# Expert weights in transfers of 4 MB into four slots instead of transfers of 2 MB into eight

## The chip, the cores and the metric

The kernel runs on one core of a Trainium2 chip. The metric is the time of one execution in microseconds of device time; the figure quoted for a kernel is the median of its runs. Arithmetic is float32 throughout. The compute engines are PE (matmul), DVE, ACT and POOL; SP only issues transfers from HBM and waits on semaphores.

## The reference

One inference step with two layers. Each layer first mixes 384 tokens (128 of a prompt, 256 of a sample) by pooling and two kinds of attention, and then sends them through a mixture of 16 experts, of which this is what matters here:

```python
def ec_moe(h, w_router, w_gate, w_up, w_down):
    b, n, d = h.shape
    cap = CAPACITY_FACTOR * n // N_EXPERTS
    aff = jax.nn.softmax(jnp.einsum('bnd,de->ben', h, w_router).astype(jnp.float32), axis=1)
    vals, idx = lax.top_k(aff, cap)
    xg = jax.vmap(lambda hb, ib: hb[ib])(h, idx)
    a = jnp.einsum('becd,edf->becf', xg, w_gate)
    u = jnp.einsum('becd,edf->becf', xg, w_up)
    o = jnp.einsum('becf,efd->becd', jax.nn.silu(a) * u, w_down) * vals[..., None].astype(h.dtype)
    return jax.vmap(lambda ib, ob: jnp.zeros((n, d), ob.dtype).at[ib.reshape(-1)].add(ob.reshape(-1, d)))(idx, o)
```

Each expert takes 16 tokens of the prompt and 32 of the sample, and has three weight matrices of 1024 x 1024, so a layer reads 16 x 3 x 4 MB = 192 MB of expert weights and uses each of them once.

## The kernel before

The program is written engine by engine, with semaphores set by hand. In each of the two layers (`l`) there are two stages.

The **mixing stage** takes its weights in 57 units of 1 MB (`w_mix`), loaded by SP at L580 into eight slots of the tensor `ring`. The last eight units fill slots 0 to 7: four of the output projection (`wo`, used by `project_out`, L1708), four of the modulation rows 10 and 11 (used by `mod`, L1439). Between them and the end of the stage stand the router, the choice of the tokens and the gathering of the chosen tokens (`gather`, L1803 and L1805).

The **expert stage** works on pairs of experts. Eight pairs make four groups (`NG`) of two pairs (`c` is 0 or 1). For a pair, PE runs six projections (`project`, L1813 to L1826): gate and up for the first 512 hidden columns (g = 0, 1), gate and up for the other 512 (2, 3), then down for each half of the output columns (4, 5). A projection has 16 matmuls: the contraction over 1024 rows in two halves (`h`), in each half four blocks of 128 rows (`q`) for two experts (`e`). Each half has its own block of 2 MB of weights, and PE waits on `landed` for it (L1818). After the first half PE raises `first_half_used`, after the second `bank_full`. Between the projections 3 and 4 stand transposes (L1840, L1846) and, in every second pair, the gathering for the next group; after projection 5 the results are spread back to the tokens (L1859), and DVE adds them to `x` (L1399).

The weights lie in 16 slots of 1 MB: slots 0 to 7 are `ring`, slots 8 to 15 lie in the tensor `M`, over buffers of the mixing stage (`more_ring`). A transfer of 2 MB (`load_double`, L547) fills a double slot, and the double slots are taken in a fixed order:

```python
EARLY = (8, 10, 12)
DOUBLES = EARLY + (0, 2, 4, 6) + (14,)
```

SP issues everything in program order. `load_early` issues the three transfers of `EARLY` when the attention's last value product is done, well before the expert stage. `load_group` issues the rest: the first transfer into 0, 2, 4, 6 waits until the two mixing units in that double slot are used, that into 14 until `x` is ready (`x_mixed`, `xss_ready`), and each later one, by `wait_pair`, until PE has used the half projection eight transfers before it. After the last transfer of a layer the same queue goes on with the mixing units of the next layer, the first of them into slot 7.

## Time and profile before

| | |
|---|---|
| median of 3 runs | 1880.3 us (1878.68 to 1880.63) |
| the profiled execution | 1879.76 us, its span 1878.0 us |
| PE busy | 1739.9 us, 93% of the span |
| DVE, ACT, POOL busy | 493.5, 296.2, 112.3 us |
| read from HBM | 528.73 MB |
| transfers of expert weights | 192 of 2048 KB |
| 16 DMA engines over the span | mean 283 GB/s, in the expert stages some 430 GB/s |

The page of the profile cuts the span into 40 slices of 47 us and gives the busy share of each engine in tenths. For TensorE it is not a measure of how close it is to its peak, since matmuls are pipelined. The line of the DMA shows the two stages well: low figures are mixing stages, a run of nines is an expert stage. The slice-by-slice view says how long an engine was busy; what it waited for is told by the views of single instructions and of the waits. Since the matmuls overlap, a group's time is read best from the distance between two starts.

### The profile page before, as it was taken

What the parts mean: (1) busy time and instruction counts of PE and PEld (TensorE: products, weight loads), DVE (VectorE), ACT (ScalarE), POOL (GpSimd) and SP (SyncE); (2) the same over time, 40 slices, a digit from 0 to 9 for tenths busy, and PEclk for the clock granted to TensorE, in tenths of its full rate; (3) what the DMA queues carried; (4) which work ended last, traced back from release to release, by engine and by line L of the source; (5) the groups of instructions that cost most, each with busy time, mean ns of one, the idle gap of its engine ahead of it and who ended that gap; (6) DMA issues with size and microseconds to landing.
All of it is one profiled execution on the core that took longest, in us unless ns stands there. A gap on an engine that the chain in (4) does not pass through costs nothing.

```text
span 1878.0 us, 18992 instructions
## 1 busy us (share of the span) xinstructions
PE 1739.9 (93%) x7336; PEld 811.0 (43%) x7336; DVE 493.5 (26%) x1126; ACT 296.2 (16%) x738; POOL 112.3 (6%) x152
## 2 busy tenths in 40 slices
PE   6998999999899998898889989999998999988997
PEld 3455555554434333242245555555544343323332
DVE  1345333212312111111114344332132121102111
ACT  2233222100201010010022333221011010101000
POOL 1151000000000000000012400000000000000000
PEclk9998999999999999999999989999999999999999
DMA  9451111642799999999982701117337999999997
GB/s 387 179 224 74 68 68 68 242 177 80 330 430 429 431 432 430 432 430 430 408 349 90 274 23 67 68 68 313 135 129 318 429 431 431 431 431 430 431 430 300
DMA packets 48080, 531.77 MB, mean 283 GB/s; under 512 B 5712, under 2 KB 6768, under 8 KB 9360
## 3 DMA queue, kind: packets, MB, share of 16 engines
q1 hardware_dynamic: 45328, 524.45, 67.2%
q0 software_dynamic: 1536, 5.87, 0.9%
q8 instruction: 44, 0.72, 0.1%
q10 hardware_dynamic: 1152, 0.56, 0.1%
q14 instruction: 20, 0.16, 0.0%
HBM read 528.73 MB, written 2.13 MB: 283 GB/s over the span
## 4 chain that ended last, share of the span: by engine, by line
PE 75%; DMA 19%; DVE 2%; ACT 2%; issue 1%; SPq 0%; ACTq 0%; POOL 0%; DVEq 0%; POOLq 0%
PE bank L1822 23%; DMA ring<-in_w_moe 14%; PE bank L1487 13%; PE bank L1506 7%; PE bank L1552 6%; PE bank L1708 4%; DMA M<-in_w_moe 4%; PE bank L1859 4%; PE bank L1439 2%; PE bank L1585 2%; PE bank L1805 2%; PE bank L1650 2%; PE bank L1515 1%; PE bank L1623 1%; PE bank L1530 1%
## 5 line engine op out<-in xcount | busy, mean ns | idle before, releaser
L1487 PE MATMUL bank<-hT,ring 128*128 128x384 f32 x768 | 260.7, 493 | 0.0
L1822 PE MATMUL bank<-M,hT 128*64 128x512 f32 x1024 | 228.0, 595 | 25.3 <-DMA M<-in_w_moe 22.1
L1822 PE MATMUL bank<-ring,hT 128*64 128x512 f32 x1024 | 226.3, 594 | 13.9 <-DMA ring<-in_w_moe 13.9
L1487 PEld LDWEIGHTS bank<-hT,ring 128*128 128x128 f32 x768 | 144.0, 191 | 105.5 <-issue 12.5
L1822 PEld LDWEIGHTS bank<-M,hT 128*64 128x64 f32 x1024 | 73.4, 137 | 175.8 <-issue 150.3
L1822 PEld LDWEIGHTS bank<-ring,hT 128*64 128x64 f32 x1024 | 73.0, 137 | 164.5 <-issue 147.1
L1506 PE MATMUL bank<-M,ring 128*128 128x384 f32 x384 | 134.2, 492 | 10.1 <-ACT M L757 10.1
L1822 PE MATMUL bank<-M 128*64 128x512 f32 x512 | 114.0, 595 | 10.6 <-DMA M<-in_w_moe 6.7
L1822 PE MATMUL bank<-ring,M 128*64 128x512 f32 x512 | 113.8, 595 | 7.9 <-DMA ring<-in_w_moe 7.2
L1552 PE MATMUL bank<-ring,hT 128*128 128x512 f32 (+1 forms) x288 | 117.4, 567 | 1.4 <-DVE hT L1028 1.4
L933 ACT ACTIVATE hT<-bank 128x512 f32<-128x512 f32 x32 | 19.1, 597 | 625.4 <-PE bank L1822 625.4
L1506 PEld LDWEIGHTS bank<-M,ring 128*128 128x128 f32 x384 | 71.0, 190 | 67.9 <-ACT M L757 19.9
L1859 PE MATMUL bank<-M 128*128 128x512 f32 x192 | 93.5, 622 | 0.0
L1708 PE MATMUL bank<-ring,xn 128*128 128x512 f32 x192 | 83.7, 594 | 2.9 <-DVE xn L1040 2.9
L1391 DVE TENSOR_TENSOR M<-bank,g2slot 128x512 f32<-128x512 f32 x32 | 22.1, 691 | 241.6 <-PE bank L1822 241.6
L1379 DVE SCALAR_TENSOR_TENSOR hT<-hT,bank 128x512 f32<-128x512 f32 x32 | 22.0, 687 | 228.7 <-ACT hT L933 228.7
L1552 PEld LDWEIGHTS bank<-ring,hT 128*128 128x128 f32 x288 | 54.2, 190 | 62.1 <-issue 62.1
L1384 DVE SCALAR_TENSOR_TENSOR hT<-hT,bank 128x512 f32<-128x512 f32 x32 | 22.0, 687 | 206.7 <-PE bank L1822 206.7
L604 POOL TENSOR_TENSOR rstd<-var,mhalf 128x8 f32<-128x8 f32 (+3 forms) x34 | 43.9, 1292 | 511.9 <-DVE var L955 511.9
L1399 DVE TENSOR_TENSOR x<-x,bank 128x512 f32<-128x512 f32 x96 | 65.9, 687 | 27.0 <-PE bank L1859 27.0
L1822 PEld LDWEIGHTS bank<-M 128*64 128x64 f32 x512 | 36.8, 137 | 81.6 <-issue 74.5
L1822 PEld LDWEIGHTS bank<-ring,M 128*64 128x64 f32 x512 | 35.9, 137 | 79.3 <-issue 67.8
(223 smaller groups left out, 1524.2 us busy)
## 6 DMA issues: line engine op xcount, KB each, us to landing
M<-in_w_moe SPq DMA_DIRECT2D x96, 2048.0 KB, 30.1
ring<-in_w_moe SPq DMA_DIRECT2D x96, 2048.0 KB, 30.1
ring<-in_w_mix SPq DMA_DIRECT2D x110, 1024.0 KB, 6.7
ring<-in_w_mix SPq DMA_DIRECT2D x4, 576.0 KB, 3.7
M<-in_counts POOLq DMA_DIRECT2D x2, 768.0 KB, 12.7
x<-in_x_sample SPq DMA_DIRECT2D x1, 1024.0 KB, 8.1
M<-in_b_mod POOLq DMA_DIRECT2D x2, 512.0 KB, 7.0
g2slot<-in_b_mod POOLq DMA_DIRECT2D x2, 512.0 KB, 10.5
```

Source lines behind the costliest of these rows:

```text
L604: nc.gpsimd.tensor_tensor(rstd[:, c0:c0 + n], var[:, c0:c0 + n], mhalf[:, 0:n], ALU.pow)\
L1399: V.tensor_tensor(xs, xs, bank[b][:, :], ALU.add).then_inc(bank_read[b], 1)
L1439: ins = mm(ps[32 * q:32 * q + 32, :], cs[:, 4 * h + q, :], w[:, q, :], start=(h == 0), stop=(h == 1))
L1487: ins = mm(ps[:, 0:TOK], w[:, q, (j % 4) * P:(j % 4 + 1) * P], hT[:, 4 * h + q, :], start=(h == 0 and q == 0), stop=(h == 1 and q == 3))
L1506: ins = mm(ps[:, 0:TOK], w[:, q, (j % 4) * P:(j % 4 + 1) * P], y[:, q, :], start=(q == 0), stop=(q == 3))
L1552: ins = mm(ps[:, 0:n], hT[:, 4 * h + q, t * P:(t + 1) * P], w[:, q, 0:n], start=(h == 0 and q == 0), stop=(h == 1 and q == 3))
L1585: ins = mm(ps[:, 0:TOK], w[:, q, g * P:(g + 1) * P], hT[:, 4 * h + q, :], start=(h == 0 and q == 0), stop=(h == 1 and q == 3))
L1650: ins = mm(ps[:, :], ckvT[:, k, t * P:(t + 1) * P], w[:, k, h * 512:(h + 1) * 512], start=(k == 0), stop=(k == 1))
L1708: ins = mm(ps[:, :], merged[:, 4 * h + q, t * P:(t + 1) * P], w[:, q, :], start=(h == 0 and q == 0), stop=(h == 1 and q == 3))
L1805: ins = mm(v[:, :, CP:USED], xn[:, t, kb * P:(kb + 1) * P], chosen(t, CP, USED), start=(t == 1), stop=(t == 2))
L1822: ins = mm(bank[b][64 * e:64 * e + 64, :], lhs(e, 4 * h + q), w[:, q, :], start=(h == 0 and q == 0), stop=(h == 1 and q == 3))
L1859: mm(bank[b][:, :], selT[:, t * P:(t + 1) * P], osb[:, n * 512:(n + 1) * 512], start=True, stop=True).then_inc(bank_full[b], 1)
```

## The change

One transfer now carries both halves of the contraction of a projection, for both experts: 4 MB, 32 KB on each of the 128 partitions where it was 16 KB. It fills four slots of 1 MB. There are four such places, taken in the order 8, 0, 4, 12; only the first (slots 8 to 11) is loaded early. PE waits once for a projection and raises only `bank_full` at its end, and SP waits for the whole projection four transfers back. The host lays the weights out so that a transfer's part for one partition is in one piece. The matmuls, their order and the number of bytes are as before.

```diff
--- before.py
+++ after.py
@@ -29,9 +29,9 @@
 UNIT = 2048
 RING = 8
 RINGX = 16
-EARLY = (8, 10, 12)
-DOUBLES = EARLY + (0, 2, 4, 6) + (14,)
-ND = len(DOUBLES)
+EARLY = (8,)
+QUADS = EARLY + (0, 4, 12)
+ND = len(QUADS)
 NEG = -1e30
 NLOAD = 8
 NPOW = 17
@@ -258,10 +258,10 @@
 
 
 LANDED = [sum(slot_of(u) == s for u in UNITS) for s in range(RINGX)]
-LANDS = [c + (12 * NP // ND if s % 2 == 0 else 0) for s, c in enumerate(LANDED)]
+LANDS = [c + (6 * NP // ND if s in QUADS else 0) for s, c in enumerate(LANDED)]
 FIRSTS = [u for u in UNITS if u[2] == 0 and u[0] in ("mod", "seg", "gate", "wo")]
 FIRST_AT = {u: n for n, u in enumerate(FIRSTS)}
-HALVES = len(FIRSTS) + 6 * NP
+HALVES = len(FIRSTS)
 
 
 def last_group(u):
@@ -524,14 +524,10 @@
             sp.dma_start(x[:, 0, :], a["x_prompt"][0]).then_inc(x_in, 16)
             sp.dma_start(x[:, 1:3, :], a["x_sample"][0].rearrange("(t p) d -> p t d", p=P)).then_inc(x_in, 16)
 
-            def wait_pair(l, gr, c, j):
-
-                g, h = j // 2, j % 2
-                if h == 0:
-                    sp.wait_ge(first_half_used, l * HALVES + len(FIRSTS) + 6 * (2 * gr + c) + g + 1)
-                else:
-                    b = (0, 1, 2, 3, 5, 6)[g]
-                    sp.wait_ge(bank_full[b], in_pair(l, b, gr, c, PROJECT[b]) + 1)
+            def wait_pair(l, gr, c, g):
+
+                b = (0, 1, 2, 3, 5, 6)[g]
+                sp.wait_ge(bank_full[b], in_pair(l, b, gr, c, PROJECT[b]) + 1)
 
             def wait_mixing(l, u):
 
@@ -540,34 +536,34 @@
                 else:
                     wait_full(sp, l, last_group(u))
 
-            def load_double(l, gr, j):
-
-                s = DOUBLES[j % ND]
-                both = more_ring[:, s - RING:s - RING + 2, :] if s >= RING else ring[:, s:s + 2, :]
-                sp.dma_start(both, a["w_moe"][l, 2 * gr + j // 12, j % 12].rearrange("p (e n) -> p e n", e=2))\
+            def load_quad(l, gr, j):
+
+                s = QUADS[j % ND]
+                four = more_ring[:, s - RING:s - RING + 4, :] if s >= RING else ring[:, s:s + 4, :]
+                sp.dma_start(four, a["w_moe"][l, 2 * gr + j // 6, j % 6].rearrange("p (e n) -> p e n", e=4))\
                     .then_inc(landed[s], 16)
 
             def load_early(l):
 
                 wait_full(sp, l, ("o", NM - 1))
                 for j in range(len(EARLY)):
-                    load_double(l, 0, j)
+                    load_quad(l, 0, j)
 
             def load_group(l, gr, first):
-                for j in range(len(EARLY) if first else 0, 24):
-                    s = DOUBLES[j % ND]
+                for j in range(len(EARLY) if first else 0, 12):
+                    s = QUADS[j % ND]
                     if j >= ND:
-                        wait_pair(l, gr, (j - ND) // 12, (j - ND) % 12)
+                        wait_pair(l, gr, (j - ND) // 6, (j - ND) % 6)
                     elif not first:
-                        wait_pair(l, gr - 1, 1, j + 12 - ND)
+                        wait_pair(l, gr - 1, 1, j + 6 - ND)
                     elif s >= RING:
                         sp.wait_ge(x_mixed, 3 * (l + 1))
                         sp.wait_ge(xss_ready, 6 * (l + 1))
                     else:
                         for u in UNITS[-RING:]:
-                            if slot_of(u) in (s, s + 1):
+                            if s <= slot_of(u) < s + 4:
                                 wait_mixing(l, u)
-                    load_double(l, gr, j)
+                    load_quad(l, gr, j)
 
             for l in range(L):
                 for n, u in enumerate(UNITS):
@@ -575,7 +571,7 @@
                     if n >= RING:
                         wait_mixing(l, UNITS[n - RING])
                     elif l > 0:
-                        wait_pair(l - 1, NG - 1, 1, 12 - ND + DOUBLES.index(s - s % 2))
+                        wait_pair(l - 1, NG - 1, 1, 6 - ND + QUADS.index(s - s % 4))
                     width = unit_width(u)
                     sp.dma_start(ring[:, s, 0:width], a["w_mix"][l, n, :, 0:width]).then_inc(landed[s], 16)
                     if n == AFTER_ATTENTION:
@@ -1812,17 +1808,15 @@
 
                     def project(g, b, lhs):
                         begin_pair(b, PROJECT[b])
+                        j = 6 * c + g
+                        s = QUADS[j % ND]
+                        pe.wait_ge(landed[s], 16 * (l * LANDS[s] + LANDED[s] + gr * (12 // ND) + j // ND + 1))
                         for h in range(2):
-                            j = 12 * c + 2 * g + h
-                            s = DOUBLES[j % ND]
-                            pe.wait_ge(landed[s], 16 * (l * LANDS[s] + LANDED[s] + gr * (24 // ND) + j // ND + 1))
                             for q in range(4):
                                 for e in range(2):
-                                    w = expert_slot(s + e)
+                                    w = expert_slot(s + 2 * h + e)
                                     ins = mm(bank[b][64 * e:64 * e + 64, :], lhs(e, 4 * h + q), w[:, q, :],
                                              start=(h == 0 and q == 0), stop=(h == 1 and q == 3))
-                            if h == 0:
-                                ins.then_inc(first_half_used, 1)
                         ins.then_inc(bank_full[b], 1)
 
                     if c == 0:
@@ -1901,11 +1895,11 @@
 
 def expert_units(v):
 
-    out = np.empty((L, NP, 6, 2, P, 2, 4, 512), np.float32)
+    out = np.empty((L, NP, 6, P, 2, 2, 4, 512), np.float32)
     for g, (name, c) in enumerate((("w_gate", 0), ("w_up", 0), ("w_gate", 1), ("w_up", 1), ("w_down", 0), ("w_down", 1))):
         w = v[name].reshape(L, NP, 2, 2, 4, P, 2, 512)[:, :, :, :, :, :, c]
-        out[:, :, g] = w.transpose(0, 1, 3, 5, 2, 4, 6)
-    return out.reshape(L, NP, 12, P, 2 * UNIT)
+        out[:, :, g] = w.transpose(0, 1, 5, 3, 2, 4, 6)
+    return out.reshape(L, NP, 6, P, 4 * UNIT)
 
 
 def kernel(**inputs):
```

On SP's queue the filling of the slots at the start of the first expert stage reads as follows, before (names: `w_moe` are the expert weights, `ring` slots 0 to 7, `M` slots 8 to 15; `bank_full` is raised by PE at the end of a projection or another group of matmuls):

```order
L547 DMA ring<-in_w_moe 128x4096 [waits bank_full2,first_half_used]
L547 DMA ring<-in_w_moe 128x4096 [waits bank_full5,first_half_used]
L547 DMA ring<-in_w_moe 128x4096 [waits bank_full6,first_half_used]
L547 DMA ring<-in_w_moe 128x4096 [waits bank_full2,first_half_used]
L547 DMA M<-in_w_moe 128x4096 [waits xss_ready,x_mixed]
L547 DMA M<-in_w_moe 128x4096 [waits first_half_used]
L547 DMA M<-in_w_moe 128x4096 [waits bank_full0]
```

and with the change:

```order
L543 DMA ring<-in_w_moe 128x8192 [waits first_half_used,bank_full5,bank_full2]
L543 DMA ring<-in_w_moe 128x8192 [waits first_half_used,bank_full2,bank_full6]
L543 DMA M<-in_w_moe 128x8192 [waits xss_ready,x_mixed]
L543 DMA M<-in_w_moe 128x8192 [waits bank_full0]
L543 DMA ring<-in_w_moe 128x8192 [waits bank_full1]
```

Four transfers into `ring` have become two, each waiting for four mixing units, and the first transfer into a reused place waits for `bank_full0` (the whole first projection) where it waited for its first half.

On PE the last projections of a pair (the first pair of the layer is shown; the slots differ from pair to pair) read before:

```order
L1822 MATMUL bank<-M 64x512 [waits landed12,bank_read6]
L1822 MATMUL bank<-M 64x512 x7
L1822 MATMUL bank<-ring,M 64x512 [waits landed0]
L1822 MATMUL bank<-ring,M 64x512 x7
```

and with the change:

```order
L1818 MATMUL bank<-ring,M 64x512 [waits landed0]
L1818 MATMUL bank<-ring,M 64x512 x15
```

Both pieces are projection 5 with its 16 matmuls: the wait for the second half is gone, and the first matmul now waits for all of the 4 MB.

On SP's queue the last expert transfer of a layer and what follows it read before:

```order
L547 ISA [waits bank_full1]
L547 DMA M<-in_w_moe 128x4096
L584 REGISTER_ALU
L584 COMPARE_AND_BRANCH
L580 DMA ring<-in_w_mix 128x2048 [waits first_half_used]
```

and with the change:

```order
L543 ISA [waits bank_full1]
L543 DMA M<-in_w_moe 128x8192
L580 REGISTER_ALU
L580 COMPARE_AND_BRANCH
L576 DMA ring<-in_w_mix 128x2048 [waits bank_full5]
```

The next layer's first mixing unit waited for the first half of projection 5 of the last pair, and now waits for the end of projection 4 (`bank_full5`).

## Rows read from the trace of the kernel before

**Rows 1.** The page: DMA share and rate in 40 slices

```profile
DMA  9451111642799999999982701117337999999997
GB/s 387 179 224 74 68 68 68 242 177 80 330 430 429 431 432 430 432 430 430 408 349 90 274 23 67 68 68 313 135 129 318 429 431 431 431 431 430 431 430 300
```

**Rows 2.** PE's groups from 650 to 920 us: line, operands, count, busy, idle before them

```profile
L1822 PE MATMUL bank<-M,hT 128*64 128x512 f32 x320 | 71.8, 595 | 11.1 <-DMA M<-in_w_moe 11.1
L1822 PE MATMUL bank<-ring,hT 128*64 128x512 f32 x318 | 70.7, 595 | 7.0 <-DMA ring<-in_w_moe 7.0
```

**Rows 3.** Issues of w_moe on SP, six stretches: start us, length

```profile
458.77 17.79 SPq L547 DMA_DIRECT2D ring<-in_w_moe  x4
...
467.45 0.33 SPq L547 DMA_DIRECT2D ring<-in_w_moe  x1
...
476.66 0.37 SPq L547 DMA_DIRECT2D M<-in_w_moe  x1
...
497.67 0.33 SPq L547 DMA_DIRECT2D M<-in_w_moe  x1
...
501.11 0.33 SPq L547 DMA_DIRECT2D M<-in_w_moe  x1
...
1429.44 0.33 SPq L547 DMA_DIRECT2D M<-in_w_moe  x1
```

**Rows 4.** PE at the end of each expert stage, in order of time

```profile
925.42 3.65 PE L1822 MATMUL bank<-ring,M 128*64 128x512 f32 x16 [1.33 <-DMA ring<-in_w_moe]
930.14 3.65 PE L1822 MATMUL bank<-M 128*64 128x512 f32 x16 [1.07 <-DMA M<-in_w_moe]
933.73 6.00 PE L1859 MATMUL bank<-M 128*128 128x512 f32 x12
939.65 1.92 PE L1439 MATMUL bank<-ring,cs 128*32 128x512 f32 x16
...
1861.84 3.65 PE L1822 MATMUL bank<-M 128*64 128x512 f32 x16 [1.08 <-DMA M<-in_w_moe]
```

**Rows 5.** Stretches: length, PE, PEld, DVE, ACT, POOL busy, PE clock, DMA share, GB/s

```profile
520.00:900.00 380.00, 353.50 (x1609) 130.16 (x1605) 67.76 (x116) 27.19 (x58) 6.87 (x14) 1.00 1.01 430
10.00:20.00 10.00, 6.22 (x27) 2.80 (x28) 2.88 (x6) 4.54 (x8) 0.87 (x1) 1.00 1.01 427
931.00:944.00 13.00, 10.58 (x42) 3.00 (x38) 4.82 (x7) 3.39 (x7) 0.00 (x0) 1.00 1.00 421
```

**Rows 6.** PE before and at the first projection of the stage, in order of time

```profile
481.99 0.29 PE L1755 MATMUL bank<-const,M 16*128 16x16 f32 x2 [3.40 <-DVE M L1318]
...
493.98 2.37 PE L1822 MATMUL bank<-M,hT 128*64 128x512 f32 x10 [1.58 <-DVE hT L1369]
```

**Rows 7.** The same view by stretches: the clock around those gaps, and the stage's end

```profile
480.00:485.00 5.00, 0.71 (x4) 0.65 (x5) 4.30 (x11) 0.00 (x0) 0.44 (x1) 0.74 0.99 421
485.00:490.00 5.00, 5.00 (x28) 5.00 (x28) 0.16 (x1) 1.40 (x4) 0.54 (x2) 0.57 0.76 324
...
925.00:930.00 5.00, 3.65 (x16) 1.26 (x16) 0.00 (x0) 0.00 (x0) 0.00 (x0) 1.00 0.68 292
```

**Rows 8.** SP's waits: total us, times, longest; and first mixing units of layer 1

```profile
SPq L547 <- PE bank L1822: 741.4, 176, 20.6
...
929.10 1.99 SPq L580 DMA_DIRECT2D ring<-in_w_mix  x4
```

**Rows 9.** PE between projections: a pair with gathering, and the last pair of a layer

```profile
680.46 0.65 PE L1840 MATMUL bank<-const,hT 128*128 128x128 f32 x4
...
688.15 10.52 PE L1822 MATMUL bank<-ring,M 128*64 128x512 f32 x48
...
702.03 5.79 PE L1859 MATMUL bank<-M 128*128 128x512 f32 x12
...
914.22 0.66 PE L1840 MATMUL bank<-const,hT 128*128 128x128 f32 x4
...
916.91 7.17 PE L1822 MATMUL bank<-ring,M 128*64 128x512 f32 x32 [0.36 <-ACT M L936]
```

## The prediction

> **What bounds the kernel now.** I began with the slices of the page. In the expert stages the 16 DMA engines are at nine tenths or more in every slice and move 429 to 432 GB/s, in the mixing stages they are mostly idle [rows 1]. The groups of PE in the later part of an expert stage say the same from the other side: the idle time in front of the projections is put down to the landing of `w_moe` [rows 2]. PE is busy 353.50 of 380 us there, and the figure counts overlapping matmuls [rows 5], so the high share of PE on the page does not make PE the bound. The stage ends when the stream of weights ends.
>
> Next, where that stream starts and ends. SP fills the eight double slots of layer 0 by 476.66, then stands until 497.67, when PE has used the first half projection, and issues the next at 501.11 [rows 3]. A half projection therefore takes 501.11 - 497.67 = 3.44 us and a whole one 6.88; PE's own row shows 3.65 for 16 records, whose modelled end overlaps the next group [rows 4]. From that first reuse at 497.67 to the start of the last half projection at 930.14 pass 432.47 us, and in layer 1 from 1429.44 to 1861.84 another 432.40 [rows 3, 4]. That is 88 transfers of 2 MB (96 of a layer less the 8 that fill the slots), 4.91 us each with the first one's latency in it. Twice the same to 0.1 us, and at an unbroken 429 to 432 GB/s between [rows 1]: each layer is *first reuse of a slot + 432.4 us + what PE does after the last landing*. The change touches all three.
>
> **The start of the stream: +3.44 us a layer.** The slots before the first reuse hold the same 16 MB. What frees a place is now the whole first projection. PE reaches it as before, since it waits there for DVE and not for weights (493.98, after 1.58 us for DVE) [rows 6], and slots 8 to 11 are loaded long before. So the first reuse is issued 3.44 us later, at 501.11 by the clock of the old trace.
>
> The filling itself changes and costs nothing as long as it is done by then. Two MB less are loaded early; the load of slots 0 to 3 waits for all of `wo` and so goes out at 467.45 where the first went at 458.77 [rows 3]; the loads of 4 to 7 and 12 to 15 go out at about 476.2 and 476.7 behind the same two waits as before. Twelve MB at 430 GB/s are 29.3 us, so the engines are done at 497 to 498, still 3 us ahead of 501.11. PE wants slots 0 to 3 at 493.98 + 6.88 = 500.9 (landed by 478), 4 to 7 at 507.7 (landed by 488) and 12 to 15 at 514.6 (landed by 499). The cover is thin for the engines and wide for PE; were the fill later than 501, the stream would start at its end instead, and each microsecond would count.
>
> **The end of the stream: +3.44 us a layer.** The last block of a layer is projection 5 of the last pair. Before, its first half ran at 925.42 while the second was on its way, and only one half, 3.44 us, followed the last landing [rows 4]. Now both halves follow it, 6.88 us. Projection 4 is no obstacle: its weights land 9.75 us before, and projection 3 with the 2.7 us of transposes behind it (914.22 to 916.91) [rows 9] is done by then to within 0.2 us. What comes after, L1859 and DVE's additions, moves along whole. In layer 0 the next layer's first `mod` stands right behind on PE (939.65) [rows 4] and needs mixing units that were issued at 929.10 [rows 8], after a small hole in the DMA (share 0.68) [rows 7]. Those now wait for projection 4 alone, which is done 2.9 us before the last landing, so the hole closes (about 1.6 us of DMA) and the units are there earlier relative to PE; PE did not wait for them before, so nothing is gained either. The later arrival of `x` is what counts, and all of layer 1's mixing stage moves with it.
>
> **The rate of the stream: -1.75 us a layer.** A transfer row per partition is 32 KB where it was 16. Rows of 16 KB go at 430 GB/s over 380 us, and at 431 in several slices of the page [rows 1, 5]; rows of 8 KB (`w_mix`) go at 427 in one stretch and at 421 in another, both with the DMA full [rows 5]. So doubling the row saved 0.8 to 2.2% of the time per byte. If what is saved is a fixed cost of a row or of a transfer, the next doubling saves half of that, 0.4 to 1.1% of the 430 us that 44 transfers take: 1.75 to 4.7 us a layer. If the saving came from something else there may be none. I take 1.75, from the stretch of 427, because it is the more careful of the two rows and the other includes the moment at which the expert weights give way to mixing units on the queue; the ends are 0 and 4.7. The Trainium skill ("DMA: Bandwidth & Descriptors", Specifications and Where 436 GB/s comes from) puts the ceiling of the ports into SBUF at 435.2 GB/s; the trace agrees as far as it goes, no slice being above 432. By that ceiling as an estimate the saving could be at most 1.1%, 4.6 us a layer.
>
> **What else moves, and costs nothing.** SP issues 96 transfers fewer, of 0.33 us each, on an engine that waited 741.4 us for PE in this place [rows 3, 8]. PE loses 96 waits and as many semaphore raises. In the middle of the stage SP may have three transfers of 9.75 us ahead of the one PE works on, 29.2 us of cover for any break of PE. The longest break is in a pair with gathering: 7.7 us from the transposes to the next projection, then 5.8 us of L1859 behind projection 5 [rows 9]. Stepped through with landings every 9.75 us, projection 3 ends 6.9 us behind its landing, projection 4 11.7, projection 5 8.8, the next pair's first 11.8. That stays far below 29.2, so the stream does not break. While PE is the slower one, early in the stage, SP's reuses follow PE's pace, which is faster than the stream, as before.
>
> **The sum.** Own time of the profiled execution 1879.76, plus 2 x (3.44 + 3.44 - 1.75) = +10.3, gives 1890.0 us. That execution lies 0.5 us below the median of the three runs, which is within their spread, so 1890 stands for the median as well. A measurement can tell about 0.2%, 3.8 us.
>
> **The rivals.**
>
> *Faster: larger rows pay in full.* If the jump from 421 to 430.5 GB/s (the middle of 430 and 431) repeats, the 430 us shrink by 2.2%, 9.5 us a layer, against 6.88 added: 2 x (6.88 - 9.5) = -5.2, 1874.5 us. It decides from a rate of about 437 GB/s on, where the two cancel. For it speaks only the row of 421; against it the row of 427 and that a fixed cost halves with each doubling. By the ceiling on the page named above it could not happen at all. Chance 0.07.
>
> *A wash.* A saving between 0.7 and 1.6% with nothing against it gives 1876 to 1884 us, within 0.2%. It needs the upper bound of the rate and a start that loses less than a half projection. Chance 0.09.
>
> *Slower still: PE's clock falls in the longer gaps.* Waiting once per 4 MB, PE stands 9.75 - 6.88 = 2.9 us in front of a projection where it stood 1.3 or less in front of a half [rows 2, 4]. In the old trace a gap of 3.40 us, with little work around it, was followed by 0.74 and 0.57 of the clock, that is, by time at 1.2 GHz [rows 6, 7], while gaps of 1.3 left it at 1.00 [rows 5]. In mid-stage the slower projections would eat up their own gap. At the end the last projection, at half clock all through, costs 6.88 more a layer: up to 1890 + 13.8 = 1903.8, and half of that if it recovers midway. Against it: the work between the gaps is dense, that around 482 was not (0.71 us of matmuls in 5) [rows 7]. The Trainium skill ("TensorE: Matmul & The Clock Gate", Why this matters for your kernels) names long idle gaps between bursts of matmuls as what lowers the clock; if 2.9 us counts as long, it gives the second of these times, and the rows of this trace have no single gap of that length before dense work. Chance 0.11.
>
> *Slower still: three transfers ahead are too few.* If PE's breaks plus SP's waits did reach 29 us, the stream would stop once per group; 3 us in three groups of two layers are 18 us, 1908. The steps above speak against it. Chance 0.03.
>
> **How the numbers follow.** My forecast has the other 0.70; its own range is 2 x (6.88 - 4.7) = +4.4 to 2 x 6.88 = +13.8, so 1884 to 1893.5. The range takes in part of the wash below (1882) and a clock that falls and recovers in the last projection above, 1897. Left out are the faster case, half of the wash and half of the two slower ones, 0.2 in all. Faster by over 0.2%: 0.07 and a little for what I have not seen, 0.08. Within 0.2%: 0.11, with the lower edge of my own range. Slower: 0.81.
>
> **What the profile after would show.** Right: SP's first transfer into a reused place comes some 3.4 us later after PE's first projection begins than before (7.1 us behind it in place of 3.7); from there to the start of the last projection 429 to 432.5 us; 6.9 us from that start to L1859; gaps of 2.9 us in front of projections late in the stage, clock 1.00; a rate of 431 to 435 GB/s; the DMA without the hole before the mixing units. Wrong: a rate outside that span, which moves the sum by 8.6 us for each per cent; a clock below 1 in the expert stage; a DMA share under 0.98 in mid-stage; or PE waiting for slots 12 to 15 at the start.

## The result, and the profile after

The changed kernel takes 1887.04 us (median of 7 runs, 1885.29 to 1888.38), the kernel before 1880.3 in the same comparison (7 runs, 1878.49 to 1883.71). The ratio is 1.0037, with a 95% interval of 1.0026 to 1.0049. It is slower by 5 to 9 us, as forecast, and by less than the 10.3 us of the sum. A second comparison of the same two kernels (`after_again`, below) gave 1.0047, 1.0034 to 1.0060. The profiled execution after took 1888.38 us, its span 1886.6.

Lines have moved: the projections are now L1818 (before L1822), the spreading back to the tokens L1853 (L1859), the transfers of expert weights L543 (L547), `mod` L1435 (L1439).

The page of the profile after, its rates in 40 slices, beside [rows 1] (its expert weights come in 96 transfers of 4096 KB):

```profile
GB/s 383 181 223 74 68 67 67 256 127 40 390 432 432 432 433 434 433 434 431 404 327 91 273 23 67 68 67 267 134 100 389 431 432 433 434 434 433 432 432 266
```

The slices of an expert stage read 431 to 434 where they read 429 to 432. The view by stretches of the same kernel (length, busy time of PE, PEld, DVE, ACT and POOL, granted clock, DMA share, GB/s) answers to [rows 5] and [rows 7]:

```profile
520.00:900.00 380.00, 355.34 (x1593) 132.66 (x1591) 67.12 (x115) 27.17 (x58) 6.86 (x14) 0.98 1.00 433
...
910.00:915.00 5.00, 2.38 (x8) 0.83 (x8) 0.69 (x1) 0.60 (x1) 0.00 (x0) 0.83 0.97 419
...
930.00:935.00 5.00, 4.13 (x22) 1.45 (x20) 0.69 (x1) 0.00 (x0) 0.00 (x0) 1.00 0.58 206
```

Three things are to be seen: 433 GB/s for 430; a granted clock of 0.98 where it was 1.00, with a stretch at 0.83 that holds the end of a wait and the start of the projection behind it (part of it at 2.4 GHz, part at 1.2 GHz); and a DMA share of 0.58 where the expert weights give way to the mixing units. Layer 1 reads the same 0.98 and 433 between 1460 and 1840 us. Below, a *dip* is such a fall of the clock within one projection. Now the two ends of the stream in order of time. SP's first transfer into a reused place, and PE at the first projection, for [rows 3] and [rows 6]:

```profile
501.98 0.33 SPq L543 DMA_DIRECT2D M<-in_w_moe  x1
```

```profile
494.86 7.09 PE L1818 MATMUL bank<-M,hT 128*64 128x512 f32 x32 [1.67 <-DVE hT L1365]
```

PE at the end of the stage, for [rows 4] and the last part of [rows 9]:

```profile
903.23 7.09 PE L1818 MATMUL bank<-M,hT 128*64 128x512 f32 x32 [2.14 <-DMA M<-in_w_moe]
912.94 8.78 PE L1818 MATMUL bank<-ring,hT 128*64 128x512 f32 x32 [2.62 <-DMA ring<-in_w_moe]
...
924.34 7.09 PE L1818 MATMUL bank<-ring,M 128*64 128x512 f32 x32 [0.36 <-ACT M L932]
932.30 7.09 PE L1818 MATMUL bank<-M 128*64 128x512 f32 x32 [0.87 <-DMA M<-in_w_moe]
939.32 6.00 PE L1853 MATMUL bank<-M 128*128 128x512 f32 x12
```

The reuse comes 501.98 - 494.86 = 7.12 us behind the first projection (before 497.67 - 493.98 = 3.69). From it to the last projection pass 932.30 - 501.98 = 430.32 us (before 432.47). From that start to L1853 pass 7.02 us (before 933.73 - 930.14 = 3.59). In all 444.46 us lie between the first projection and L1853, against 439.75 before: +4.71 in this layer. Layer 1 gives 444.38 against 439.67, again +4.71. So the trace accounts for +9.4 us in the two expert stages. The measure *first projection to L1859 (L1853)* is used for every kernel below, since the rest of the time scatters by itself and its code hardly differs between them.

### The profile page after: what moved, and what is told of

It reads as the page before. It is cut to its first block, busy times and chain, and to the rows that moved or that the text cites. A ratio compares the mean times of both kernels' runs of the same rounds, so it can differ in the third digit from the quotient of the medians.

```text
span 1886.6 us, 18662 instructions
## 1 busy us (share of the span) xinstructions
PE 1751.1 (93%) x7336; PEld 821.2 (44%) x7336; DVE 493.9 (26%) x1126; ACT 295.9 (16%) x738; POOL 112.2 (6%) x152
## 4 chain that ended last, share of the span: by engine, by line
PE 74%; DMA 20%; DVE 2%; ACT 2%; issue 1%; SPq 0%; ACTq 0%; POOL 0%; DVEq 0%; POOLq 0%
PE bank L1818 22%; DMA ring<-in_w_moe 16%; PE bank L1483 13%; PE bank L1502 7%; PE bank L1548 6%; PE bank L1704 4%; PE bank L1853 4%; DMA M<-in_w_moe 3%; PE bank L1435 2%; PE bank L1581 2%; PE bank L1801 2%; PE bank L1646 2%; PE bank L1511 1%; PE bank L1619 1%; PE bank L1526 1%
## 5 line engine op out<-in xcount | busy, mean ns | idle before, releaser
L1818 PE MATMUL bank<-M,hT 128*64 128x512 f32 x1024 | 241.1, 627 | 30.2 <-DMA M<-in_w_moe 26.9
L1818 PE MATMUL bank<-ring,hT 128*64 128x512 f32 x1024 | 227.1, 597 | 8.3 <-DMA ring<-in_w_moe 8.3
L1818 PEld LDWEIGHTS bank<-M,hT 128*64 128x64 f32 x1024 | 80.1, 143 | 187.5 <-issue 174.4
L1818 PEld LDWEIGHTS bank<-ring,hT 128*64 128x64 f32 x1024 | 75.7, 138 | 157.1 <-issue 149.8
L1818 PE MATMUL bank<-ring,M 128*64 128x512 f32 x512 | 113.3, 595 | 8.1 <-DMA ring<-in_w_moe 7.4
L1818 PE MATMUL bank<-M 128*64 128x512 f32 x512 | 113.1, 594 | 7.3 <-ACT M L932 3.9
L1853 PE MATMUL bank<-M 128*128 128x512 f32 x192 | 93.6, 622 | 0.0
L1818 PEld LDWEIGHTS bank<-ring,M 128*64 128x64 f32 x512 | 36.6, 137 | 78.7 <-issue 67.6
L1818 PEld LDWEIGHTS bank<-M 128*64 128x64 f32 x512 | 37.1, 137 | 77.1 <-issue 74.4
```

The source lines that it names most:

```text
L1818: ins = mm(bank[b][64 * e:64 * e + 64, :], lhs(e, 4 * h + q), w[:, q, :], start=(h == 0 and q == 0), stop=(h == 1 and q == 3))
L1853: mm(bank[b][:, :], selT[:, t * P:(t + 1) * P], osb[:, n * 512:(n + 1) * 512], start=True, stop=True).then_inc(bank_full[b], 1)
```

## The experiments

Each kernel's stage length is read off its trace as above, layer 0 and layer 1. "Mixing" is the time from the start of the span to the first projection of layer 0 plus that from L1859 to the first projection of layer 1. Ratios are to the kernel before, timed on the same chip.

| kernel | stage 0, stage 1, us | mixing, us | GB/s | ratio (95% interval) |
|---|---|---|---|---|
| before | 439.75, 439.67 | 986.0 | 430.6 | |
| changed | 444.46, 444.38 | 985.2 | 432.6 | 1.0037 (1.0026 to 1.0049) |
| after_again | 444.34, 444.55 | 983.2 | 432.6 | 1.0047 (1.0034 to 1.0060) |
| e1_wait_whole | 446.76, 448.32 | 983.2 | 430.6 | 1.0081 (1.0067 to 1.0095) |
| e5_rows16 | 448.07, 448.22 | 982.8 | 430.6 | 1.0082 (1.0065 to 1.0099) |
| e6_rows8 | 444.07, 444.16 | 984.3 | 426.3 | 1.0049 (1.0035 to 1.0064) |
| e2_tail | 441.67, 441.76 | 982.1 | 432.8 | 1.0022 (1.0012 to 1.0032) |
| e3_start | 444.20, 444.72 | 982.4 | 432.3 | 1.0046 (1.0033 to 1.0060) |
| e8_start_loop | 442.16, 444.07 | 986.6 | 432.5 | 1.0045 (1.0028 to 1.0062) |
| e4_both | 442.29, 440.09 | 981.6 | 432.4 | 1.0011 (1.0002 to 1.0020) |
| e9_both_loop | 441.07, 439.81 | 986.7 | 432.7 | 1.0002 (0.9993 to 1.0012) |
| e7_warm | 450.78, 450.77 | 984.8 | 432.5 | 1.0112 (1.0095 to 1.0129) |
| e12_early | 440.78, 440.99 | 984.0 | 432.3 | 1.0003 (0.9994 to 1.0012) |
| e13_early_warm | 439.83, 439.88 | 982.8 | 432.2 | 1.0001 (0.9992 to 1.0009) |

(GB/s: from 20 us behind the first reuse to 20 us before the last projection's start, the mean of the two layers; the last digit moves by 0.1 to 0.3 with the way in which packets at the edges are counted.)

**e1_wait_whole: the waits of the change without its transfers.** In the kernel before, PE waits for both halves first, and SP for the whole projection:

```diff
                         for h in range(2):
                             j = 12 * c + 2 * g + h
                             s = DOUBLES[j % ND]
                             pe.wait_ge(landed[s], ...)
+                        for h in range(2):
+                            s = DOUBLES[(12 * c + 2 * g + h) % ND]
                             for q in range(4):
...
-                if h == 0:
-                    sp.wait_ge(first_half_used, l * HALVES + len(FIRSTS) + 6 * (2 * gr + c) + g + 1)
-                else:
-                    b = (0, 1, 2, 3, 5, 6)[g]
-                    sp.wait_ge(bank_full[b], in_pair(l, b, gr, c, PROJECT[b]) + 1)
+                b = (0, 1, 2, 3, 5, 6)[g]
+                sp.wait_ge(bank_full[b], in_pair(l, b, gr, c, PROJECT[b]) + 1)
```

Expected:

> The kernel before, its 2 MB transfers and eight slots kept, but PE waits for both halves of a projection before its first matmul, and SP takes a place again only after the whole projection. The theory (a late start and a late end of the stream, 3.44 us each and layer, less a rate that the larger rows raise) expects all of the loss and none of the gain: 2 x 6.88 = +13.8 us, 1894, with 430 to 431 GB/s in mid-stage, the first reuse 7.1 us behind PE's first projection and 6.9 us from the last landing to L1859. If the loss were due to the four places or the size of the transfers, this kernel would stay at 1880. If the rate has nothing to do with the row size, it comes out where the changed kernel did, at 1887.

Measured: 1893.77 us against 1878.56, +15.2. Stage 0 grew by 7.0 us (two half projections, 6.88, were expected), stage 1 by 8.65. The rate did not move. Both ends show in its trace, here the last projection of each layer (L1821 are its projections, L1858 the spreading):

```profile
931.82 3.65 PE L1821 MATMUL bank<-ring,M 128*64 128x512 f32 x16 [2.82 <-DMA M<-in_w_moe]
...
938.84 3.59 PE L1858 MATMUL bank<-M 128*128 128x512 f32 x7
```

```profile
1869.60 5.31 PE L1821 MATMUL bank<-ring,M 128*64 128x512 f32 x16 [2.63 <-DMA M<-in_w_moe]
...
1878.28 1.98 PE L1858 MATMUL bank<-M 128*128 128x512 f32 x4
```

In layer 0 the last projection takes 7.02 us, in layer 1 8.68: its first half began at a lowered clock, 5.31 us for 3.65. So the waits alone cost what the theory says, and the 1.66 us more is the price of a dip where it falls on the last projection.

**e5_rows16 and e6_rows8: what the rate hangs on.** e5 is the changed kernel with each 4 MB in HBM as two pieces of 16 KB per partition:

```diff
-                sp.dma_start(four, a["w_moe"][l, 2 * gr + j // 6, j % 6].rearrange("p (e n) -> p e n", e=4))\
+                sp.dma_start(four.rearrange("p (h e) n -> p h (e n)", h=2),
+                             a["w_moe"][l, 2 * gr + j // 6, j % 6].rearrange("h p n -> p h n"))\
                     .then_inc(landed[s], 16)
```

> The changed kernel, each 4 MB still one transfer into the same four slots, but laid out in HBM as two pieces of 16 KB for each partition instead of one of 32 KB. If the rate gain is a cost per row (per packet), mid-stage falls back from 432.6 to 430.6 GB/s and the stream of each layer grows by 2 us: about +4 us against the changed kernel. If it is a cost per transfer (its end on each of the 16 engines), the rate stays at 432.6 and so does the time.

e6 is the kernel before with each 2 MB as two pieces of 8 KB:

```diff
-                sp.dma_start(both, a["w_moe"][l, 2 * gr + j // 12, j % 12].rearrange("p (e n) -> p e n", e=2))\
+                sp.dma_start(both, a["w_moe"][l, 2 * gr + j // 12, j % 12].rearrange("e p n -> p e n"))\
                     .then_inc(landed[s], 16)
```

> The kernel before with its transfers of 2 MB, each now two pieces of 8 KB for a partition instead of one of 16 KB. From 430.6 GB/s with 16 KB and 432.6 with 32 KB a fixed cost of 5.6 ns per row follows (0.0225 us on each 2 MB for four rows of an engine fewer). Eight rows more then make 4.915 us in place of 4.870 per transfer: 426.6 GB/s, 4.0 us more a layer, 8 us over the kernel before. If the gain of the larger row was peculiar to 32 KB, the rate stays at 430.6 and the time too.

The view by stretches, first of e5, then of e6:

```profile
520.00:900.00 380.00, 353.38 (x1579) 131.61 (x1579) 67.13 (x115) 27.17 (x58) 6.86 (x14) 0.98 1.01 431
```

```profile
520.00:900.00 380.00, 350.06 (x1593) 128.62 (x1591) 67.78 (x116) 27.19 (x58) 6.87 (x14) 1.00 1.01 426
```

e5 kept the size and number of the transfers and fell back to the old rate: the gain belongs to the row of 32 KB, not to the transfer of 4 MB. Its stage is 448.1, with a dip on the last projection in both layers (its own +4 us over the changed kernel had left the dips out; measured were +6.7, of which two dips are 3.4). Without the dips it is 446.4, against e1's 446.7: the change from the other side, where the coarse waits cost some 14 us and the longer rows give 4.3 back. That its time, 1893.75, is e1's to the tenth is chance, since e1 had the dip in one layer only. e6 came out at 426.3 GB/s where 426.6 was worked out, its stage 4.4 us longer a layer (4.0 expected), 1887.32 us. Both runs also put the pieces of a row at other places in HBM, so length and place are not separated; for the length speaks that the rate of the third size was foretold from the other two. Three sizes of row lie on one line, with a fixed cost of about 5.8 ns per row on its DMA engine (worked out in the last section).

**e2_tail: the last 4 MB of a layer in two transfers.**

```diff
-                    load_quad(l, gr, j)
+                    if last and j == 11:
+                        for h in range(2):
+                            load_half(l, gr, j, h)
+                    else:
+                        load_quad(l, gr, j)
...
                         for h in range(2):
+                            if h and type(gr) is int and gr == NG - 1 and c == 1 and g == 5:
+                                pe.wait_ge(landed[14], 16 * (l + 1))
```

> The changed kernel, with the last 4 MB of each layer as two transfers of 2 MB, for whose second PE waits between the halves. The theory expects 3.44 us a layer back: 1887.0 - 6.9 = 1880.2, with the last half projection 3.6 us before L1859. If the end of the stage does not bound (PE late for other reasons), nothing comes back: 1887.

Measured: 1882.4 us, ratio 1.0022; the stage is 2.7 us shorter than the changed kernel's, not 3.44. The trace says why (L1833 are its projections, L1868 the spreading):

```profile
909.94 7.09 PE L1833 MATMUL bank<-ring,hT 128*64 128x512 f32 x32 [0.93 <-DMA ring<-in_w_moe]
...
919.65 7.09 PE L1833 MATMUL bank<-ring,M 128*64 128x512 f32 x32 [0.36 <-ACT M L945]
926.56 7.04 PE L1833 MATMUL bank<-M 128*64 128x512 f32 x32
933.53 6.00 PE L1868 MATMUL bank<-M 128*128 128x512 f32 x12
```

The last projection no longer waits. Projection 4, still one block of 4 MB, is in front of it, and from its start two whole projections run to the end, 13.88 us. It cannot start before its weights land (919.51; the row names ACT, which was done at the same moment), 9.7 us ahead of the last landing (929.19); so L1868 stands at least 13.88 - 9.7 = 4.2 us behind the last landing, against some 7.0, and 2.8 us is all that this repair can give.

**e3_start and e8_start_loop: the first reuse by halves.** e3 writes the first group of PE out so that its first half projection can release a place; e8 splits the fifth transfer of every group and leaves the loop as it is:

```diff
+                    if j == ND:
+                        sp.wait_ge(first_half_used, l * HALVES + len(FIRSTS) + gr + 1)
+                        load_half(l, gr, j, 0)
+                        wait_pair(l, gr, 0, 0)
+                        load_half(l, gr, j, 1)
+                        continue
```

> The changed kernel, with the first reused place filled by two transfers of 2 MB, the first issued after the first half projection. The stream of the changed kernel stands from 498.8 to about 502.5 us, so starting 3.44 us earlier just closes that hole: the theory expects 3.2 to 3.4 us a layer back, 1880.4. If the stream has slack in it and its start does not matter, 1887.

> The start repair of e3_start once more, but the first group of PE is not written out: every group splits its fifth transfer, so that PE keeps its loop. e3 gave nothing back; its trace shows 9 reads of 16 KB of instructions in mid-stage where the changed kernel has 5, with a landing 0.5 to 1.1 us late behind several of them. The theory (extra instruction reads hold up one of the 16 DMA engines and with it the whole stream by 0.6 us each) expects them back at 5 and first projection to L1859 at 442.4 us a layer in place of 444.4 (the hole that can be closed is 1.9 to 2.3 us), some 4 us under the changed kernel. If the start of the stream simply does not matter, 444.4 again.

In both, the reuse is issued 3.69 us behind the first projection, as in the kernel before. SP's first two transfers into a reused place in e8_start_loop, where the first projection starts at 496.15:

```profile
499.84 3.76 SPq L552 DMA_DIRECT2D M<-in_w_moe  x2
```

e3 gained 0.3 us in layer 0 (444.20) and lost 0.3 in layer 1 (444.72, with a dip of 1.5 us on its last projection), e8 gained 2.3 us in layer 0 (442.16) and, with a dip on its last projection (8.71 us in place of 7.02), 0.3 in layer 1. A bound of some 2 us, where 3.4 was expected, comes from the fill. In the changed kernel the records of the DMA show the last of the fill's packets over at 501.00 and the next stream's first at 502.94, a hole of 1.94 us, and only the hole can be closed, however early the reuse is issued. In the ten stages that reuse a whole place behind such a fill (the changed kernel twice, e2, e5 and e7) it is 1.5 to 3.2 us. The expectation of e3 had it from 498.8 to 502.5: that is when most of the engines stand, but the last one works until 501.00. Why e3 lost the gain again is shown only in part. Its PE program has one group more written out in place of a pass of the loop, and the DMA view from 520 to 900 us counts 9 reads of instructions (0.15 MB) in e3 and 5 (0.08 MB) in e8, as in the changed kernel.

Landings in e3's layer 0 are 9.7 us apart, but 10.8 at 549.6, 10.2 at 869.7 and 10.8 at 899.8, each 3 to 7 us after a read of 16 KB of instructions (546.4, 864.0, 892.9). With the loop restored the extra reads are gone, and stage 0 is 2.0 us shorter, stage 1 0.8 when the dips are taken off. Four reads of 0.6 us each, all on the engine that is last, would make 2.4. But a read alone does not delay a landing: in the changed kernel no landing behind its 5 reads is more than 0.1 us late, and in e8's layer 1, with the loop, one is (11.1 us for 9.7, at 1486.2). The records do not name the engine either, so this stays a possible cause and not a shown one. In the times of the whole kernels (1886.98 and 1887.45) the difference is lost in the mixing stages, which took 982.4 us in e3's trace and 986.6 in e8's.

**e4_both and e9_both_loop: both repairs.** e4 is e2 and e3 together, e9 the loop form of both (its last transfer is split in every group).

> The changed kernel with both repairs at once. The theory says that the two losses add and that the rate gain of 2.15 us a layer is then left alone: 1887.0 - 13.5 = 1873.5, about 7 us under both kernels (4.3 us of the rate and what the medians differ from the trace). If the two repairs share their gain (the one hides the other), about 1880.

> Both repairs in loop form. The theory expects the two to add now: 442.4 less the 2.7 us that the tail repair gave, 439.7 a layer from the first projection to L1859, the same as the kernel before. If the repairs share their gain, 441.7.

e4: 1881.0 us, stages 442.3 and 440.1. e9: 1879.25 us, 441.1 and 439.8, where 439.7 was expected; ratio 1.0002. The two repairs add: 2.3 and 2.8 us in layer 0, where e9 gained 3.4 with a dip of 1.4 in it, and 2.0 (e8's dip taken off) and 2.6 in layer 1, where it gained 4.6. With them the kernel is level with the one before. The two layers of e9 differ by 1.26 us, and projection 3 of the last pair shows why, behind the same gap once with a dip and once without; e4's 442.29 and 440.09 have the same cause:

```profile
911.66 8.51 PE L1841 MATMUL bank<-ring,hT 128*64 128x512 f32 x32 [2.63 <-DMA ring<-in_w_moe]
...
1844.04 7.09 PE L1841 MATMUL bank<-ring,hT 128*64 128x512 f32 x32 [2.62 <-DMA ring<-in_w_moe]
```

Once the tail is repaired, PE waits for no weights between a dip in this projection and the end of the stage, so the dip is no longer hidden. The forecast for e4, 1873.5, was wrong in its sizes: 6.9 us for each repair, where 4 to 5 and 5.5 were there to be had.

**e7_warm: keeping the clock up.** Three further matmuls stand in front of the waits of projections 2 and 3; they compute nothing that is used.

```diff
+                        for k in range(3 if g in (2, 3) else 0):
+                            mm(bank[b][64:128, :], xn[:, 0, 0:64], xn[:, 1, 0:512], start=True, stop=True)
                         pe.wait_ge(landed[s], ...)
```

> The changed kernel, with three further matmuls into the free bank in front of the waits of projections 2 and 3 of each pair, whose result the projection overwrites; nothing of the output depends on them. In the changed kernel the projection behind the longest gap takes 8.7 us in place of 6.9 at a granted clock that dips to about 0.83. The theory says that the dip is hidden, since the next weights land only after it: with it gone (clock 1.00 in the stage) the time stays, within 1 us. If the dip costs, each of some 7 dips gives 1.8 us back, up to 12 us.

The clock stayed at 1.00, and the kernel took 1899.6 us, 21.3 more than the one before on its chip, and some 13 more than the changed one, whose stages it exceeds by 6.3 and 6.4 us. The experiment says little on the dips: the three matmuls took 2.6 us before each of two projections, which brought a pair of experts to 57.7 us on PE (the mean of 60.1 with gathering and 55.3 without), where the stream takes 6 x 9.7 = 58.2. So PE, which starts behind the stream, never caught up: it waits for no weights from the first projection to the last, and the stage is as long as PE's own work. Neither theory had that.

**e12_early and e13_early_warm: all repairs at once.** e12 is e9 with the first half of slots 12 to 15 loaded early again:

```diff
                 for j in range(len(EARLY)):
                     load_quad(l, 0, j)
+                load_half(l, 0, 3, 0)
...
-                    if j == 11:
-                        for h in range(2):
+                    if j in (3, 11):
+                        for h in range(1 if first and j == 3 else 0, 2):
```

e13 adds two idle-filling matmuls, as in e7 but two instead of three.

> e9_both_loop, and the fourth transfer is split as well: its first 2 MB go into slots 12 and 13 with the early load, as in the kernel before. The fill is then over some 4 us before the first reuse, so that the start repair is worth its full 3.44 us and not the 2.2 of e8. The theory expects, from PE's first projection to L1859, 444.4 - 3.44 - 2.7 = 438.3 us a layer (before: 439.7), plus 1.7 where the clock dips in the last projections, and a time 1 to 3 us under the kernel before. If what bound e9 was something else than the end of the fill, 439.7 and no difference to before.

> e12_early with two idle-filling matmuls in front of the waits of projections 2 and 3 of each pair (e7_warm had three, took 2.6 us for them and so made PE late; two take 1.7 and leave a gap of 0.9). The theory expects no dip of the clock (1.00), PE on time in the last pair, the tail repair at its full 3.44 us, and 437.5 us a layer: 2 x (437.5 - 439.7) = -4.4 us against the kernel before. If the dips cost nothing in the tail, the same as e12; if PE is late again, 3 us or more over e12.

e12: 1878.99 us, 440.8 and 441.0. e13: 1877.94 us, 439.8 and 439.9; both level with before (1878.61). PE at the end of layer 0, first in e12 and then in e13 (L1842 and L1844 are the projections):

```profile
909.47 8.47 PE L1842 MATMUL bank<-ring,hT 128*64 128x512 f32 x32 [2.62 <-DMA ring<-in_w_moe]
...
920.56 7.09 PE L1842 MATMUL bank<-ring,M 128*64 128x512 f32 x32 [0.36 <-ACT M L952]
```

```profile
907.84 7.09 PE L1844 MATMUL bank<-ring,hT 128*64 128x512 f32 x32 [0.91 <-DMA ring<-in_w_moe]
...
917.64 7.09 PE L1844 MATMUL bank<-ring,M 128*64 128x512 f32 x32 [0.45 <-DMA ring<-in_w_moe]
```

Here too the dip is seen to cost. In e12 projection 3 takes 8.4 us behind a gap of 2.62, and projection 4 starts when PE is free; in e13 it takes 6.9 and projection 4 waits for its weights. The stages of the two kernels differ by 0.95 and 1.1 us. The rest of what I expected is not there: the fill is over early (holes of 3.8 and 3.4 us before the reuse), yet e13 is at 439.85 and not at 437.5. The tail gives 0.6 less by e2's bound. Every fourth block now has rows of 16 KB, which gives up a quarter of the rate gain, 0.55 us. About 1 us a layer stays open; one landing a layer that is 0.5 to 0.6 us late in e13's trace (10.29 us behind the one before at 558.9, 10.20 at 1770.9, where 9.7 is usual) makes about half of it.

**after_again: the changed kernel once more.**

> The changed kernel once more. From the first projection to L1859 the theory expects 444.4 us in each layer, 1.7 more where the clock dips in the last projection, with 432.5 GB/s. The mixing stages are the same code as before; whatever else the medians show (+6.7 us in the first comparison against +9.4 by the stage) is then their scatter, and this comparison should fall between +6.5 and +11 us.

444.34 and 444.55 us, 1887.08 us against 1878.61: +8.5, in the range that was given.

## Why the prediction was right

*The bound.* The stream of weights ends the stage: right. The changed kernel's stage moved by what its ends and its rate moved by, to the tenth in both layers: 3.43 + 3.43 - 2.15 = 4.71.

*The start, +3.44 a layer.* Measured 7.12 - 3.69 = 3.43. Right, on thinner ground than I said. I had the fill over at 497 to 498, 3 us ahead of the reuse at 501.1; in fact it took 32.8 us from 468.2 instead of 29.3 and was over at 501.0, under one microsecond ahead of 501.98. A 12 MB fill at the mean rate leaves out its start (the first packet begins 0.98 us behind the issue) and the slowest engine at its end (from 499.3 on most of the engines stand). PE, as said, waited for none of the three places.

*The end, +3.44 a layer.* Measured 7.02 - 3.59 = 3.43. Right in its size. Two details were wrong. Projection 3 of the last pair had a dip in layer 0, so projection 4 started 1.8 us behind its landing, and the last projection's wait of 0.87 us is all that was left to hide it. And the hole in the DMA before the mixing units did not close: the first of them was issued at 931.47, 0.7 us before the last landing and not 2.9, and the share in that place is 0.58 (before 0.68). PE still waited for none of them, so it cost nothing here.

*The rate, -1.75 a layer.* This term was too small: 430.32 and 430.24 us for 432.47 and 432.39, so -2.15. I had taken the ratio of [rows 5] with 427 GB/s for rows of 8 KB; e6 measured 426.3 with expert weights alone. That a doubling saves half of the one before was right: 8 to 16 KB 1.0%, 16 to 32 KB 0.5%. With the measured value the sum is +9.4.

*The cover in mid-stage.* Right: no break of the stream, SP's three transfers ahead were enough.

*The remainder.* +9.4 in the stages against +6.7 in the first pair of medians and +8.5 in the second. The rest must lie in the mixing stages. They are the same code, but for the wait in front of the first mixing units, and take from 981.6 to 986.7 us over the traces above. One piece of it is the same `mod` in layer 1, in the kernel before and then in the changed one, at two clocks:

```profile
1404.63 3.29 PE L1439 MATMUL bank<-ring,cs 128*32 128x512 f32 x16
```

```profile
1409.58 1.92 PE L1435 MATMUL bank<-ring,cs 128*32 128x512 f32 x16
```

The first ran at a granted clock of 0.72 in its stretch (1403 to 1409), the second at 1.00 (1408 to 1413). Whether anything of the 1 to 3 us is systematic, 14 traces with one execution each do not tell.

*The rivals.* The faster one is out: by e6 and e5 the saving halves with each doubling. The wash is out by both intervals; its own figures did not fit each other either, since a saving of 0.7 to 1.6% against the full 6.88 us gives 1887.5 to 1879.8 and not 1876 to 1884. The clock did fall, as the third rival said and my forecast did not; a clock below 1 stood on my list of what would show the forecast wrong. Behind gaps of 2.1 to 2.6 us ten projections of the changed kernel took 8.7 us for 7.0, five in each layer (670.64, 738.57, 786.89, 854.82, 912.94 and 1605.44, 1673.36, 1721.68, 1789.60, 1837.99). In this kernel the dips are hidden, because the last projection was never among them in its two traces and behind any other PE waits for weights again before the stage ends. That is luck and not mechanism: in e5 the last projections, behind gaps of 2.59 and 2.55 us, both had one. Where one falls on the last projection (e1, e5, e3, e8) it costs 1.5 to 1.7 us, not 6.88: it recovers in the first half. With a dip in both layers the stages would have given +12.8, still between the ends of my range (+4.4 to +13.8). The Trainium skill ("TensorE: Matmul & The Clock Gate", Why this matters for your kernels) names long idle gaps; the trace agrees that a gap of 2.6 us can be long enough. It shows too that it need not be: the last projection of layer 1, behind 2.55 us, ran at full speed.

```profile
1867.06 7.09 PE L1818 MATMUL bank<-M 128*64 128x512 f32 x32 [2.55 <-DMA M<-in_w_moe]
```

## What to carry to other kernels

Where a stream from HBM bounds a stage, its length was here the start of the reuse, the bytes by the rate, and the work behind the last landing; the larger block lengthened both ends by what PE takes for the added part, once per stage, and gained only on the rate. Measure the rate by the row that one partition receives, not by the transfer: the same 4 MB in rows of 16 KB had none of the gain. And before mending an end, look at the block in front of it and at what fills the buffer before: here they left 2.8 of 3.4 us to be had at one end and about 2 at the other. A repair can also uncover what the old wait had hidden, as the dips in the last pair of e9 and e12 show.

## What the runs showed of the hardware

- The rate of transfers into 128 partitions with the DMA full: 426.3 GB/s with rows of 8 KB, 430.6 with 16 KB, 432.6 with 32 KB, with 16 KB the same in transfers of 2 MB and of 4 MB (e1, e5). With the rate shared by 16 engines, one row takes its engine 307.5, 608.8 and 1212.0 ns. A fixed 5.8 ns and 301.5 ns per 8 KB give 307.3, 608.8 and 1211.8. Without the fixed part the rate would by this estimate be 16 x 8192 / 301.5 = 434.7 GB/s. The Trainium skill ("DMA: Bandwidth & Descriptors", Where 436 GB/s comes from) states a ceiling of 435.2; the runs agree, no mean over a stage being above it.
- The granted clock can fall in the middle of dense work behind a gap of 2.1 to 2.6 us, for 1.7 us of lost time, and not each time: in the changed kernel behind ten such gaps and not behind four others (641.61, 903.23, 1576.41, 1867.06). In the kernel before, whose gaps in the stage are 1.3 us at most behind the first projection, and in e13 it stayed at 1.00.
- Reads of instructions (16 KB each) stand among the packets of the same 16 DMA engines as the weights; writing out one of four groups of PE's loop took them from 5 to 9 in 380 us.
